# Two matmuls at a time on different halves of TensorE's array: key scores, index scores and latent output products issued in pairs

## What is computed

```python
# first block, feed-forward: every token asks 8 heads x 2 half queries of 64 for the best of 128 keys
q = (xb @ wq).reshape(C, 8, 2, 64)
s = jnp.einsum('chpd,hpnd->chpn', q, keys)          # key scores
sv, si = lax.top_k(s, 16)                           # then the best 16 experts of each head, a gather, a sum
# second block: which keys a query may see is chosen by 8 index heads of 64
s_idx = jax.nn.relu(jnp.einsum('btjd,bsd->btjs', q_idx, k_idx))     # index scores
s_idx = jnp.einsum('btjs,btj->bts', s_idx, w_idx)
_, idx = lax.top_k(s_idx, 128)
# attention in a latent space of 128, 16 heads; what a head found is then taken from 128 to 64
logits = jnp.einsum('bthc,btkc->bthk', q_lat, c_sel) - slopes * dist
o_lat = jnp.einsum('bthk,btkc->bthc', softmax(logits), c_sel)
o = jnp.einsum('bshc,hcd->bshd', o_lat, w_uv)       # latent output product
```

## Time and profile before

| | |
|---|---|
| median of three runs | 2329.91 us (2326.18 to 2331.55) |
| profiled execution: own time | 2328.31 us |
| its span in the trace | 2326.5 us |
| PE busy | 2185.0 us (94%) |
| DVE busy | 1522.5 us (65%) |
| ACT busy | 1010.3 us (43%) |
| POOL busy | 1028.4 us (44%) |
| key scores, eight blocks | 389.0 to 660.8 us |
| index scores | 1706.7 to 1730.9 us |
| latent attention | 2080.9 to 2217.5 us |

### The profile page before, as it was taken

How to read it: one execution, slowest core, us unless ns; L and a number is a source line. 1 busy time by engine, 2 the same in 40 slices (tenths; PEclk the granted TensorE clock), 3 DMA queues, 4 the chain that set the end, 5 groups by cost and what they waited for, 6 DMA issues and landing times.

```text
span 2326.5 us, 31263 instructions
## 1 busy us (share of the span) xinstructions
PE 2185.0 (94%) x11543; PEld 1919.3 (82%) x11543; DVE 1522.5 (65%) x2894; ACT 1010.3 (43%) x1857; POOL 1028.4 (44%) x575
## 2 busy tenths in 40 slices
PE   6899999999999978999999999999899979999998
PEld 6754678999999978999999999999767768876676
DVE  3678465768999637777778777776458844017724
ACT  3244533336878833333333333333336652236621
POOL 4210044565656555565465656463314444430042
PEclk9999899999999999999999999999889989999998
DMA  4100022466777878889798888795212222220021
GB/s 170 56 28 1 1 82 91 160 209 234 287 269 260 310 267 294 331 311 324 267 345 296 325 321 317 273 341 175 100 37 82 73 81 100 91 81 1 1 73 55
DMA packets 141591, 414.09 MB, mean 178 GB/s; under 512 B 13056, under 2 KB 57728, under 8 KB 139648
## 3 DMA queue, kind: packets, MB, share of 16 engines
q1 hardware_dynamic: 104576, 277.86, 34.5%
q0 software_dynamic: 36864, 134.23, 15.5%
HBM read 370.62 MB, written 41.42 MB: 177 GB/s over the span
## 4 chain that ended last, share of the span: by engine, by line
PE 79%; DVE 11%; ACT 4%; issue 3%; DMA 2%; POOL 0%; DVEq 0%; SPq 0%; ACTq 0%; POOLq 0%
PE bank L441 21%; PE bank L442 20%; PE bank L443 20%; PE bank L732 4%; PE bank L884 2%; DVE tmp L2112 1%; PE bank L589 1%; DVE co L1603 1%; DMA wraw<-in_wstream 1%; PE wide L461 1%; PE bank L903 1%; PE bank L554 1%; PE wide L893 1%; PE wide L903 1%; PE wide L527 1%
## 5 line engine op out<-in xcount | busy, mean ns | idle before, releaser
L2244 POOL TENSOR_TENSOR wl<-wraw,wh 128x1024 fp32r<-128x1024 f32 x275 | 679.0, 2471 | 938.6 <-ACT wh L987 929.5
L441 PE MATMUL bank<-XH,wh 128*128 128x384 f32 (+2 forms) x1840 | 669.7, 364 | 49.0 <-issue 22.2
L442 PE MATMUL bank<-XL,wh 128*128 128x384 f32 (+2 forms) x1840 | 658.9, 358 | 0.0
L443 PE MATMUL bank<-XH,wl 128*128 128x384 f32 (+2 forms) x1840 | 654.4, 356 | 0.0
L987 ACT CAST wh<-wraw 128x1024 fp32r<-128x1024 f32 x362 | 377.7, 1046 | 238.4 <-PE bank L443 214.3
L441 PEld LDWEIGHTS bank<-XH,wh 128*128 128x128 f32 x1840 | 354.6, 193 | 95.3 <-issue 60.1
L442 PEld LDWEIGHTS bank<-XL,wh 128*128 128x128 f32 x1840 | 355.3, 193 | 28.6 <-issue 2.2
L443 PEld LDWEIGHTS bank<-XH,wl 128*128 128x128 f32 x1840 | 355.5, 193 | 27.9
L441 PE MATMUL bank<-WTH,wh 128*128 128x384 f32 x1024 | 349.6, 341 | 18.5 <-issue 13.0
L443 PE MATMUL bank<-WTH,wl 128*128 128x384 f32 x1024 | 347.1, 339 | 0.0
L442 PE MATMUL bank<-WTL,wh 128*128 128x384 f32 x1024 | 347.1, 339 | 0.0
(11 more groups left out here) (404 smaller groups left out, 2934.5 us busy)
## 6 DMA issues: line engine op xcount, KB each, us to landing
wraw<-in_wstream SPq DMA_DIRECT2D x362, 512.0 KB, 3.9
g_scratch<-gs SPq DMA_DIRECT2D x12, 2048.0 KB, 7.5
gr<-g_scratch SPq DMA_DIRECT2D x15, 1536.0 KB, 15.0
a_scratch<-tmp SPq DMA_DIRECT2D x72, 192.0 KB, 2.0
tmp<-a_scratch SPq DMA_DIRECT2D x46, 192.0 KB, 7.3
sq<-a_scratch SPq DMA_DIRECT2D x26, 192.0 KB, 7.1
h<-in_hT SPq DMA_DIRECT2D x8, 264.0 KB, 5.8
fetched<-in_u_rows,diag POOLq DMA_INDIRECT x128, 7.0
```

The source lines that it names most:

```text
L441: pe.matmul(o, w1, x1, start=n == 0, stop=False)
L442: pe.matmul(o, w1, x2, start=False, stop=False)
L443: m = pe.matmul(o, w2, x1, start=False, stop=n == len(ks) - 1)
L2244: return pool.tensor_tensor(lo, src, hi.bitcast(F32), ALU.subtract)
```

## The change

In all three places two products that use different halves of the array stand next to each other. Nothing is computed that was not computed before, and no product has another shape.

- Key scores: within a block the loop over the halves p is now inside that over the four heads.
- Index scores: heads go in pairs (2k, 2k + 1), and for each query tile the even and the odd head stand next to each other (`HEAD_PAIRS`). ReLU results go in turn through five buffers (`RELUED`) in place of three. The steps of the latent keys stand at other units: they come after units 6, 12 and 18 on PE (before: 3, 9 and 15), the sum over squares and the diagonals on DVE both after unit 8 (before: 3 and 9), the scaling after unit 14 (before: 9).
- Latent output: the product of an even head is no longer issued after its own last values but directly ahead of the product of the odd head after it.

```diff
+    HEAD_PAIRS = [(2 * pair + p, qt) for pair in range(4) for qt in range(1, 4) for p in range(2)]
+    RELUED = [tmp[1], tmp[2], sq[0], rb, tmp[0]]
@@ key scores, PE
-                for p in range(2):
...
-                    for i in range(4):
-                        hd = half * 4 + i
+                for i in range(4):
+                    hd = half * 4 + i
+                    for p in range(2):
                         mm = pe.matmul(wide[0][:, p * 512 + i * 128:p * 512 + i * 128 + 128],
@@ index scores, PE
-        for j in range(8):
-            if j % 2:
-                next(latent_steps, None)
-            p0 = 64 * (j % 2)
-            for qt in range(1, 4):
-                n = 128 * (qt + 1)
+        for pair in range(4):
+            if pair > 0:
+                next(latent_steps)
+            for qt, j in [(qt, 2 * pair + p) for qt in range(1, 4) for p in range(2)]:
+                p0, n = 64 * (j % 2), 128 * (qt + 1)
                 bank = next_bank(("idx", j, qt), (relued, (j, qt)))
@@ latent output, PE
-            if 0 <= n - 6 < len(UNITS2) and UNITS2[n - 6][1] == 3:
+            if 0 <= n - 6 < len(UNITS2) and UNITS2[n - 6][1] == 3 and UNITS2[n - 6][0] % 2:
+                out_head(UNITS2[n - 6][0] - 1)
                 out_head(UNITS2[n - 6][0])
@@ index scores, ACT
-        for j in range(8):
-            if j == 1:
+        for n, (j, qt) in enumerate(HEAD_PAIRS):
+            if n == 2:
                 act.wait_ge(*idx_out.at(("ckv",)))
                 square(sq[1][:, 0:512], ckvT[:, :], "ckv", 0)
...
+            if n == 8:
                 roots("ckv", 512)
-            if j == 5:
+            if n == 18:
...
+            act.wait_ge(*idx_mm.at(j, qt))
+            if n > 4:
+                act.wait_ge(*summed.at(*HEAD_PAIRS[n - 5]))
@@ index scores, DVE
-        for j in range(8):
-            if j == 1:
+        for n, (j, qt) in enumerate(HEAD_PAIRS):
+            if n == 8:
                 statistic("ckv", 512, wide[1], 0, 128, 2, after=("fin", 3))
-            if j == 3:
                 diagonals("ckv", 512, 2, after="kx")
+            if n == 14:
                 dve.wait_ge(*bcast.at("ckv"))
```

More of the change, by code:

```diff
@@ L698, in route @@
             for half in range(2):
-                for p in range(2):
[L700 to L708, removed]
-                    for i in range(4):
-                        hd = half * 4 + i
+                if tt == 0 and half == 0:
+                    pe.wait_ge(*rb_ready.at("ffn"))
+                    pe.wait_ge(*qp_made.at(7))
+                    pe.wait_ge(*ld_ky.at("ky"))
+                    pe.wait_ge(*xtok_out.at("sbuf"))
+                if half == 1:
+                    pe.wait_ge(*routed.at(tt, "replaced", 0))
+                if half == 0 and tt > 0:
+                    pe.wait_ge(*routed.at(tt - 1, "replaced", 1))
+                for i in range(4):
+                    hd = half * 4 + i
+                    for p in range(2):
                         mm = pe.matmul(wide[0][:, p * 512 + i * 128:p * 512 + i * 128 + 128],
@@ L817, in tensor @@
         latent_steps = latent_keys()
-        for j in range(8):
-            if j % 2:
-                next(latent_steps, None)
-            p0 = 64 * (j % 2)
-            for qt in range(1, 4):
-                n = 128 * (qt + 1)
+        pe.wait_ge(*idx_out.at("kx2"))
+        pe.wait_ge(*idx_out.at(("qi", 3)))
+        for pair in range(4):
[3 more added lines that the diff above has]
+                p0, n = 64 * (j % 2), 128 * (qt + 1)
                 bank = next_bank(("idx", j, qt), (relued, (j, qt)))
-                if j == 0 and qt == 1:
-                    pe.wait_ge(*idx_out.at("kx2"))
-                    pe.wait_ge(*idx_out.at(("qi", 3)))
                 pe.matmul(bank[:, 0:n], qi[p0:p0 + 64, j // 2, qt * 128:qt * 128 + 128], kx[p0:p0 + 64, 0:n],
@@ L1351, in scalar @@
         act.copy(ckvT[:, :], bank_of[("ckv",)][:, :]).then_inc(*idx_out.tell(("ckv",)))
-        for j in range(8):
-            if j == 1:
+        for n, (j, qt) in enumerate(HEAD_PAIRS):
+            if n == 2:
                 act.wait_ge(*idx_out.at(("ckv",)))
                 square(sq[1][:, 0:512], ckvT[:, :], "ckv", 0)
+            if n == 4:
+                act.wait_ge(*idx_mm.at("wx"))
+            if n == 8:
                 roots("ckv", 512)
-            if j == 5:
+            if n == 18:
                 act.wait_ge(*idx_mm.at("ckv_t"))
@@ L1361, in scalar @@
                          bank_of["ckv_t"][:, :].rearrange("p (j c) -> p j c", c=128)).then_inc(*idx_out.tell(("ckv_t",)))
[L1362 to L1369, removed]
+            act.wait_ge(*idx_mm.at(j, qt))
+            if n > 4:
+                act.wait_ge(*summed.at(*HEAD_PAIRS[n - 5]))
+            act.activation(RELUED[n % 5][:, 0:128 * (qt + 1)], bank_of["idx", j, qt][:, 0:128 * (qt + 1)],
+                           ACT.Relu).then_inc(*relued.tell((j, qt)))
         def branch_in(c):
@@ L2072, in vector @@
                                          ALU.mult).then_inc(*idx_step.tell("ckvn"))
[L2073 to L2082, removed]
+            u, so = RELUED[n % 5][:, 0:128 * (qt + 1)], sidx[qt - 1][:, :]
+            dve.wait_ge(*relued.at(j, qt))
+            if j == 0:
+                dve.wait_ge(*idx_out.at(("wx",)))
+                dve.tensor_scalar(so, u, wx[:, qt, 0:1], None, ALU.mult).then_inc(*summed.tell((j, qt)))
+            else:
+                dve.wait_ge(*summed.at(j - 1, qt))
+                dve.scalar_tensor_tensor(so, u, wx[:, qt, j:j + 1], so, ALU.mult,
+                                         ALU.add).then_inc(*summed.tell((j, qt)))
         for qt in range(1, 4):
```

## The result

The changed kernel takes **2306.98 us** (median of 5 runs, 2303.97 to 2314.79); the kernel before takes 2329.91 in the same comparison (5 runs). The ratio is 0.9907, with a 95% interval of 0.9889 to 0.9925. The forecast was 2309, range 2303 to 2318. The profiled execution has a span of 2304.3 us against 2326.5.

What follows compares the result with a forecast made beforehand. PE, busy 94% of the span, was taken to bound the kernel. Key scores 4.3, index scores 7.3 and latent output 9.2 sum to 20.8 us off 2328.3, or 2307.5; plus 1.6 for the median gives 2309 us, range 2303 to 2318.

Steps and rivals of the forecast that it cites:

- Key scores, 4.3 us: Key scores: halves overlap through the whole block, 1.1 us in place of 1.64, eight blocks save 4.3 us (bounds 0 to 6.0).
- Index scores, 7.3 us: Index scores: pairs shorten the stage by 8.0 us (bounds 5.4 to 9.9), less 0.7 given back, so 7.3 us.
- the 0.7 for the product behind: Product after the index scores: it may begin at half clock, costing 1.8 us with chance 0.4, counted as 0.7.
- PE needs 2.14 us for six units, DVE becomes the limit: Index scores: with pairs PE takes 2.14 us per six units at full clock, so DVE's accumulations, about 14 us, limit.
- Does it last: Branch behind the index scores: its start moves with the stage, DVE is not late, PE's 8.8 us wait keeps its length.
- Latent output, 9.2 us: Latent attention: column halves run fully side by side, 1.19 us saved by each of eight pairs, less 0.3 at the end.
- The second case: Latent output: both products run one after the other with one change of form, 0.33 us saved a pair, 2.6 us in all.
- In turn: Rival, latent output: column halves run one after the other, 14.2 us saved in all, 2315.7 us; chance 0.20.
- The clock: Rival, index scores: clock drops for the stage and the product behind, 2.0 us in place of 7.3, 2314.4; chance 0.08.
- Index gain lost behind DVE: Rival, index scores: DVE's accumulations end after the copy of `("xr", 0)`, 2316.4 us; chance 0.05.
- No gain in blocks: Rival, key blocks and index pairs: halves overlap no more than today, only the latent term is left, 2320.7 us; chance 0.04.
- Draining at each change of half: Rival, key and index scores: each change of half drains the array, 11 us slower, 2341 us; chance 0.03.

Runs made afterwards that it cites:

- the fourth run: All three edits as in the changed kernel, but index heads issued one after another: 2303.09 us, ratio 0.9892 to before, index scores 15.49 us.
- the two runs above: Index heads one after another against the changed kernel: new places with three buffers, index scores 15.82 us; old places with five buffers, 24.14 us.

## Why the prediction was right, and where it was not

**The bound.** Right. PE's microseconds were the chain's microseconds in all three stages, and no wait ate them: the waits for routing and gating are 4.7 and 5.1 us (4.7 and 5.2 before), the wait in the branch 8.8.

**Key scores, 4.3 us.** The mechanism was right (the same half gives 1.98), and the block too: 1.1 forecast, 1.09 measured. The term measured 3.1. Seven blocks gained 0.55 each; the one behind PE's wait of 4.2 us ran at half clock, took 2.00 and gained nothing. But the block is not the whole of it: the step that was left out of the term is the clock of the stage, which differs from one execution to the next. The stage had 6.8 us at half clock before and 10.2 after. In two of the later executions that block ran at full clock, and all eight took 1.09; the stage still took 268.5, again with 10.2 us at half clock, at other places. Where the time at half clock is the same (13.7 us: 273.6 in the kernel with the index edit alone, 269.6 and 269.7 in two with paired keys) the pairs save 3.9.

**Index scores, 7.3 us.** The time measured is 9.4, near the upper bound of 9.9 (which should read 10.1: 1730.98 less 1720.9), and the 0.7 for the product behind did not fall due, since the clock stayed full. But the step "PE needs 2.14 us for six units, DVE becomes the limit", which put the gain down to the pairs, is the one that failed. Six units take 2.50 us in pairs, not 2.14, and 2.97 in order at full clock, not twice 2.14, since the order of before already let one head's rows run beside the other's at each change of half. So PE could save 0.47 for each pair of heads, 1.9 in all. It saves 0.7: DVE sets the time of the scaling of `ckvT`, which begins 10.9 us behind the start of the stage with pairs and 11.1 without, and PE hands 1.3 us back as longer waits (2.1 for 0.8). The price of neighbours that read each other was too low, 0.64 for 0.56, so 0.08. Measured, such an accumulation starts 0.10 us behind the end of the one ahead, where the others start 0.08 before it (DVE's timeline of the changed kernel and of the fourth run): 0.19 each. What the edit brought came from the places of the latent steps: 3.3 us of waits and 5.0 of clock, by the two runs above. The forecast had the wait for the diagonals and the clock among its limits and priced neither by itself, and it left out the first wait, 1.3 us for ACT's square. That 7.3 came near 9.4 is luck: without a single pair the stage gained 8.75, in the fourth run. The bounds held because they were worked out from PE's end at either clock, whatever brings it.

**Does it last.** Right: the start of the branch moved with the stage, by 12.8 us in all, the 139.0 us up to the end of the wait stayed, and the 8.8 us kept their length. That DVE would not be late held by 0.61 us only; in the fourth run, without pairs, it had 3.7.

**Latent output, 9.2 us.** Right in mechanism and size: 9.5 measured, 1.19 for each of seven pairs (1.19 forecast) and 1.15 at the end (0.9 forecast). The second case, one change of form less for 2.6 us, is what the run with the same half shows: 15.83 us for two heads, 0.33 saved. The rule weighed there (the Trainium skill, "TensorE: Matmul & The Clock Gate", Part 3: a weight load overlaps matmuls in flight only if their row groups differ) would have given that second case. The measured 1.01 us for two products on the same rows and different columns contradicts it here: in the pair behind 2110.1 us all four weight loads start within 0.06 us, while the first rows of both products run, and these start 0.01 us apart. The speed-up for column tiles in the same part agrees in kind; no run here has three of them.

**The rivals.** In turn: no, by 1.01 us. The clock: no, it went the other way. Index gain lost behind DVE: no, by 0.61 us. No gain in blocks: no. Draining at each change of half: no, a change of half saves 0.13 to 0.34 us on average.

The total came close for a reason beside the argument as well: key scores 1.2 too much, index scores 2.1 too little, output 0.3 too little, and the stretches that nothing changed moved by +3.1, -3.3, +1.0 and -0.9. Two errors of opposite sign and drifts that cancel are luck, not a forecast.

## What to carry to other kernels

Two small matmuls that leave half of the array idle should stand next to each other on different halves, of rows or of columns; groups of two products to a half do almost as well, and what is saved is one product's columns and one change of form. Before putting a gain down to the headline of an edit, keep its new places and undo only its new order: here the places of three small steps in other engines' queues were worth 8.4 us of 9.4, the buffers 0.3 and the pairs 0.7. And count what a wait costs twice, once for itself and once for the clock behind it, but check in the windows whether that clock really falls.

## What the runs showed of the hardware that I had not expected

- The clock went to half behind short waits inside the index scores: in four of five executions behind the 1.3 us for ACT, in all four from the 2.3 to 2.8 us for the diagonals on (in one of them it had been half since the first wait), but not behind a wait of 1.37 us at another place.
- Products on the two column halves, which need all the same rows, overlap as fully as products on two row halves: 4 rows in 1.01 us, where the same 4 rows on one half take 1.86.
- A change of half lets about three rows overlap (0.34 us with rows of 128 columns), not a whole following group: 1.64 us for one change in sixteen rows, 1.19 for three, 1.09 for seven.
- An accumulation on DVE (128x512) took 2.70 us where it began 0.6 us behind the start of POOL's split of a weight tile, and 0.75 where it began ahead of it. Pairing PE's products shifted the two onto each other.
- The same code ahead of the key scores took 387.9 to 401.6 us in thirteen profiled executions, with 47.8 to 85.3 us of it at half clock. A single time of this kernel tells less than any of its stages.
